# A two-block transformer kernel: the final norm of the first block folded into the second block's norm, and one of two attention maps weighed on VectorE instead of GpSimd

## What is computed

```python
# end of the first block
x = x + 0.5 * _swiglu(_rmsnorm(x, ffn2_norm), ffn2_w_gate, ffn2_w_up, ffn2_w_down)
x = _rmsnorm(x, final_norm)             # x * rsqrt(mean(x*x) + 1e-6) * gain
# start of the second block
h = _rms_norm(x, norm_g) * (1.0 + scale[:, None, :]) + shift[:, None, :]
dq, dk, dv, cq, ckv, kr, g = jnp.split(h @ w_in, cuts, axis=-1)
# its end
out = (mixed * jax.nn.silu(g)) @ w_out
return x + gate[:, None, :] * out
```

## Time and profile before

| what | value |
| --- | --- |
| median of 3 runs | 1967.73 us |
| the profiled execution: its own time | 1971.7 us |
| its span | 1969.9 us |
| mean granted TensorE clock | 0.961 |
| PE busy | 1844.2 us (94%) |
| DVE, ACT, POOL busy | 1042.8, 624.5, 97.8 us |
| first attention | about 518.5 to 716 us |
| last FFN matmul to the first slot's end | about 1523 to 1578 us |
| slots up to the second attention | to about 1750 us |
| gate and output projection | about 1858 to 1970 us |

### The profile page before, as it was taken

How to read it: one execution, slowest core, us unless ns; L and a number is a source line. 1 busy time by engine, 2 the same in 40 slices (tenths; PEclk the granted TensorE clock), 3 DMA queues, 4 the chain that set the end, 5 groups by cost and what they waited for, 6 DMA issues and landing times.

```text
span 1969.9 us, 22640 instructions
## 1 busy us (share of the span) xinstructions
PE 1844.2 (94%) x9109; PEld 1393.0 (71%) x9109; DVE 1042.8 (53%) x1597; ACT 624.5 (32%) x975; POOL 97.8 (5%) x148
## 2 busy tenths in 40 slices
PE   7999999999888899998999999999999499899888
PEld 6888888878555568755788888888887254365667
DVE  6665453465354445358644357534545655656753
ACT  4221221321256641024322233212223255324620
POOL 0000000000134420000000000000000000011100
PEclk8999998999699999999999999999999699799989
DMA  6545322362000012031333233233323022111221
GB/s 203 186 145 196 107 86 59 103 197 69 1 1 1 1 44 76 17 101 43 97 96 96 98 91 107 84 99 107 99 80 111 27 91 86 38 44 33 76 74 54
DMA packets 234908, 163.59 MB, mean 83 GB/s; under 512 B 10317, under 2 KB 225589, under 8 KB 234677
## 3 DMA queue, kind: packets, MB, share of 16 engines
q1 hardware_dynamic: 232484, 157.95, 26.3%
q10 hardware_dynamic: 2320, 4.20, 0.6%
HBM read 155.84 MB, written 6.29 MB: 82 GB/s over the span
## 4 chain that ended last, share of the span: by engine, by line
PE 83%; DVE 11%; issue 2%; POOL 2%; ACT 2%; DMA 0%; SPq 0%; ACTq 0%; DVEq 0%
PE bank L860 23%; PE bank L861 22%; PE bank L862 22%; PE bank L1070 2%; DVE bank L1745 2%; PE bank L1209 2%; POOL Pm L497 2%; PE bank L1060 2%; PE bank L1094 1%; DVE rout L1835 1%; PE bank L1155 1%; PE bank L1147 1%; PE bank L937 1%; PE bank L930 1%; PE bank L1324 1%
## 5 line engine op out<-in xcount | busy, mean ns | idle before, releaser
L860 PE MATMUL bank<-h_hi,w_hi 128*128 128x512 f32 x1216 | 492.4, 405 | 16.4 <-DVE h_lo L1467 12.3
L862 PE MATMUL bank<-h_hi,w_lo 128*128 128x512 f32 x1216 | 477.3, 393 | 0.0
L861 PE MATMUL bank<-h_lo,w_hi 128*128 128x512 f32 x1216 | 477.2, 392 | 0.0
L554 ACT ACTIVATE w_hi<-w_raw 128x2048 fp32r<-128x2048 f32 (+3 forms) x134 | 236.8, 1767 | 630.7 <-PE bank L862 567.8
L1404 DVE TENSOR_TENSOR w_lo<-w_raw,w_hi 128x2048 fp32r<-128x2048 f32 (+3 forms) x134 | 282.4, 2108 | 58.6 <-ACT w_hi L554 55.8
L860 PEld LDWEIGHTS bank<-h_hi,w_hi 128*128 128x128 f32 x1216 | 231.2, 190 | 94.0 <-issue 40.6
L861 PEld LDWEIGHTS bank<-h_lo,w_hi 128*128 128x128 f32 x1216 | 231.3, 190 | 53.0 <-issue 6.4
L862 PEld LDWEIGHTS bank<-h_hi,w_lo 128*128 128x128 f32 x1216 | 230.5, 190 | 49.3
L860 PE MATMUL bank<-u_hi,w_hi 128*128 128x512 f32 x352 | 138.0, 392 | 0.0
L861 PE MATMUL bank<-u_lo,w_hi 128*128 128x512 f32 x352 | 137.8, 392 | 0.0
L862 PE MATMUL bank<-u_hi,w_lo 128*128 128x512 f32 x352 | 137.6, 391 | 0.0
(11 more groups left out here) (352 smaller groups left out, 2548.4 us busy)
## 6 DMA issues: line engine op xcount, KB each, us to landing
w_raw<-in_w_in SPq DMA_DIRECT2D x28, 1024.0 KB, 5.2
w_raw<-in_ffn_w_gate SPq DMA_DIRECT2D x44, 512.0 KB, 3.7
w_raw<-in_ffn_w_up SPq DMA_DIRECT2D x44, 512.0 KB, 4.8
w_raw<-in_ffn_w_down SPq DMA_DIRECT2D x32, 704.0 KB, 4.5
ada_w<-in_ada_w SPq DMA_DIRECT2D x16, 768.0 KB, 6.3
w_raw<-in_w_in SPq DMA_DIRECT2D x21, 512.0 KB, 3.9
w_raw<-in_w_out SPq DMA_DIRECT2D x8, 1024.0 KB, 5.0
w_raw<-in_w_branch_nsa SPq DMA_DIRECT2D x8, 512.0 KB, 5.0
```

The lines of the kernel that those rows point to most:

```text
L554: act.activation(w_hi[s % 2][:, 0:n], w_raw[s % 2][:, 0:n], ACT.Copy).then_inc(s_hi, 1)
L860: pe.matmul(o, l[0], r[0], start=first, stop=False)
L861: pe.matmul(o, l[0], r[1], start=False, stop=False)
L862: return pe.matmul(o, l[1], r[0], start=False, stop=last)
```

## The change

**Part 1, the norm.** With g the final gain, e = 1e-6 and r the product of both inverse roots, r = 1/sqrt(mean((g*g+e)*x*x) + e*e). ACT therefore squares x times sqrt(g*g+e) (`G_ROOT`) first, then plain, then writes `xg` = x times gain times scale (`G_OUT`). From the weighted sum comes std = 1/r by one root, and DVE forms h = xg + std*shift, which is the wanted h times std. The projections behind it are linear, so their tiles are multiplied by r when they are emptied: `scale_tile` in place of `copy_tile` in slots 0 to 11, `scale_rows` for `dv`, and for the gate a DVE pass before ACT's silu. `xg` lies in the place of `h_lo`. The normed x itself, needed only at the end, is made in slots 2 (inverse root) and 10 to 17 (one `final_tile` each).

**Part 2, the bias matmuls.** The eight inside `first_tiles` move behind it, into slot 0.

**Part 3, the first attention.** POOL weighs the first map of a unit, DVE the second (`weigh_second`); `p_ready` comes after POOL's one instruction, and the transposes of the second map wait for a new signal `p1_ready`.

```diff
+G_EPS2, G_ROOT, G_OUT = 120, 0, 8
+        xg = at("xg", [P, KD, S], F32, base[0] - KD * S * 4)
...
                 pool.wait_ge(sem("sum_ready"), attended(u))
-                for i in range(2):
-                    p_ = Pm[u % 2][:, i, 0:n]
-                    ins = pool.tensor_scalar(p_, p_, mstat[:, u % 2, 6 + i:7 + i], gates[:, t, g0 + 3 * i:g0 + 3 * i + 1], ALU.mult, ALU.mult)
-                ins.then_inc(sem("p_ready"), 1)
+                p_ = Pm[u % 2][:, 0, 0:n]
+                pool.tensor_scalar(p_, p_, mstat[:, u % 2, 6:7], gates[:, t, g0:g0 + 1], ALU.mult, ALU.mult).then_inc(sem("p_ready"), 1)
... (ACT, square)
-                act.activation((sq_w if n == 2 else sq)[k % 2][:, :], x[:, k, :], ACT.Square).then_inc(sem("nsq"), 1)
                 if n == 3:
-                    act.activation(sqg[k % 2][:, :], x[:, k, :], ACT.Square, scale=col[:, G_FIN + k:G_FIN + k + 1]).then_inc(sem("nsqg"), 1)
+                    act.activation(sqg[k % 2][:, :], x[:, k, :], ACT.Square, scale=col[:, G_ROOT + k:G_ROOT + k + 1]).then_inc(sem("nsqg"), 1)
+                act.activation((sq_w if n == 2 else sq)[k % 2][:, :], x[:, k, :], ACT.Square).then_inc(sem("nsq"), 1)
+                if n == 3:
+                    act.activation(xg[:, k, :], x[:, k, :], ACT.Copy, scale=col[:, G_OUT + k:G_OUT + k + 1]).then_inc(sem("xg_ready"), 1)
... (ACT, big_norm(3))
+                    act.wait_ge(sem("gmm"), 1)
+                    act.activation(std[:, :], bank[6][:, :], ACT.Sqrt, bias=col[:, G_EPS2:G_EPS2 + 1], scale=1.0 / D).then_inc(sem("token_std"), 1)
... (ACT)
-            act.wait_ge(sem("gsum_ready"), 1)
-            act.activation(std[:, :], tmp[:, :], ACT.Sqrt, bias=col[:, G_EPS:G_EPS + 1], scale=1.0 / D).then_inc(sem("nstd"), 1)
... (ACT, zg)
-                act.wait_ge(acc_full, a + 1)
-                if i >= 2:
-                    act.wait_ge(acc_free, a - 1)
-                act.activation(gate_out[i % 2][:, :], bank[a % 4][:, :], ACT.Silu).then_inc(sem("zg_ready"), 1)
                 if i == 0:
                     norm_sqrt(26, 3, slice(0, P), 128)
+                act.wait_ge(acc_free, a + 1)
+                act.activation(gate_out[i % 2][:, :], gate_out[i % 2][:, :], ACT.Silu).then_inc(sem("zg_ready"), 1)
... (PE, turn)
                 for i in range(maps):
+                    if i:
+                        pe.wait_ge(sem("p1_ready"), attended(u))
... (PE, beside)
-                if slot < BIAS_SLOTS and slot:
+                if slot < BIAS_SLOTS:
                     bias_four()
-                if slot == 1:
+                if slot < 2:
                     bias_four()
+                if slot == 21:
+                    pe.wait_ge(sem("rs_ready"), 4)
+                    pe.wait_ge(sem("rope_done"), 22)
+                    for t in range(NT):
+                        ins = pe.matmul(bank[4][:, t:t + 1], rsx[0:1, t * P:(t + 1) * P], ones[0:1, 0:1], start=True, stop=True)
+                    ins.then_inc(sem("rst_full"), 1)
-                    first_tiles(wh, wl, ..., (h_hi, h_lo), ("h_ready", 24), bias_four)
+                    first_tiles(wh, wl, ..., (h_hi, h_lo), ("h_ready", 24))
... (DVE, final_norm)
-                dve.wait_ge(sem("nstd"), 4)
-                done(dve.reciprocal(rs[:, :], std[:, :]), "rs_ready")
-                dve.wait_ge(sem("gmm"), 1)
-                done(dve.tensor_mul(tmp[:, :], bank[6][:, :], rs[:, :]))
-                done(dve.tensor_mul(tmp[:, :], tmp[:, :], rs[:, :]), "gsum_ready")
-                final_tile(0)
-                dve.wait_ge(sem("nstd"), 5)
-                done(dve.reciprocal(rs2[:, :], std[:, :]), "rs_ready")
+                dve.wait_ge(sem("token_std"), 1)
                 for k in range(KD):
-                    if k:
-                        final_tile(k)
-                    done(dve.scalar_tensor_tensor(t, x[:, k, :], col[:, G_MOD + 8 + k:G_MOD + 9 + k], rs2[:, :], ALU.mult, ALU.mult))
-                    tick(dve.tensor_scalar(t, t, col[:, G_MOD + k:G_MOD + k + 1], None, ALU.add), "hn_ready")
+                    dve.wait_ge(sem("xg_ready"), k + 1)
+                    tick(dve.scalar_tensor_tensor(t, std[:, :], col[:, G_MOD + k:G_MOD + k + 1], xg[:, k, :], ALU.mult, ALU.add), "hn_ready")
                     if k:
                         low3(k - 1)
                 low3(KD - 1)
+                done(dve.reciprocal(rsx[:, :], std[:, :]), "rs_ready")
... (DVE, first attention)
+            def weigh_second(u):
+                dve.wait_ge(sem("sum_ready"), attended(u))
+                tick(dve.tensor_scalar(p_, p_, mstat[:, u % 2, 7:8], gates[:, t, g1:g1 + 1], ALU.mult, ALU.mult), "p1_ready")
                     sums(u, 2)
+                    weigh_second(u)
                 if u + 2 < U0:
                     peaks(u + 2)
... (DVE, evacuate)
-                copy_tile(dst, n)
+                if t is not None:
+                    scale_rows(dst, t, 256)
+                elif slot < 12:
+                    scale_tile(dst)
+                else:
+                    copy_tile(dst)
...
+                if slot == 2:
+                    dve.wait_ge(sem("nstd"), 4)
+                    done(dve.reciprocal(rsf[:, :], rsf[:, :]))
+                if 10 <= slot < 18:
+                    final_tile(slot - 10)
+                if slot == 21:
+                    dve.wait_ge(sem("rst_full"), 2)
+                    done(dve.tensor_copy(col[:, G_RST:G_RST + NT], bank[4][:, 0:NT]))
... (DVE, gate)
+            scale_tile(gate_out[0][:, :])
             inverse(5)
             for m in range(KD):
-                take()
+                if m + 1 < KD:
+                    scale_tile(gate_out[(m + 1) % 2][:, :])
                 dve.wait_ge(sem("zg_ready"), m + 1)
-                free(dve.tensor_mul(tmp[:, :], (diff_out + latent_out)[m], gate_out[m % 2][:, :]))
+                done(dve.tensor_mul(tmp[:, :], (diff_out + latent_out)[m], gate_out[m % 2][:, :]))
```

More of the change, by code:

```diff
@@ L588, in work @@
                 def work(i, a):
+                    if n == 3 and i == 1:
+                        act.wait_ge(sem("root_ready"), 1)
+                        act.wait_ge(sem("gain_out"), 2)
                     if i and n < 3:
@@ L598, in deviation @@
                     act.wait_ge(sem("rs_ready"), n)
-                act.activation((std_w if n == 2 else std)[:, :], bank[5][:, :], ACT.Sqrt, bias=col[:, G_EPS:G_EPS + 1], scale=1.0 / D).then_inc(sem("nstd"), 1)
+                act.activation((std, std, std_w, rsf)[n][:, :], bank[5][:, :], ACT.Sqrt, bias=col[:, G_EPS:G_EPS + 1], scale=1.0 / D).then_inc(sem("nstd"), 1)
             def big_norm(n):
@@ L666, in prepare @@
                     act.activation(cosM, ang[1][:, :], ACT.Sin).then_inc(sem("trig_ready"), 1)
+                if i == 17:
+                    act.wait_ge(sem("root_in"), 1)
+                    act.activation(col[:, G_ROOT:G_ROOT + KD], col[:, G_ROOT:G_ROOT + KD], ACT.Sqrt).then_inc(sem("root_ready"), 1)
             ffn("ffn1", 1)
@@ L900, in big_norm @@
             def big_norm(n):
+                if n == 3:
+                    pe.wait_ge(sem("sqg_added"), 7)
+                    pe.matmul(bank[6][:, :], ones, sqgsum[:, :], start=True, stop=True).then_inc(sem("gmm"), 1)
                 pe.wait_ge(sem("sq_added"), 7 * n + 7)
@@ L904, in big_norm @@
                 pe.matmul(bank[5][:, :], ones, (sqsum_w if n == 2 else sqsum)[:, :], start=True, stop=True).then_inc(sem("nmm"), 1)
-                if n == 3:
-                    pe.wait_ge(sem("sqg_added"), 7)
-                    pe.matmul(bank[6][:, :], ones, sqgsum[:, :], start=True, stop=True).then_inc(sem("gmm"), 1)
             def norm_sum(weights, quarter, start, stop, again=False):
@@ L1280, in _ @@
                 if s == 0:
-                    first_tiles(wh, wl, ((0, slice(0, P)), (0, slice(P, 2 * P))), (h_hi, h_lo), ("h_ready", 24), bias_four)
+                    first_tiles(wh, wl, ((0, slice(0, P)), (0, slice(P, 2 * P))), (h_hi, h_lo), ("h_ready", 24))
                     beside()
@@ L1423, in add_square @@
                 s_, t_ = (sq_w, sqsum_w) if n == 2 else (sq, sqsum)
+                dve.wait_ge(sem("dve_seq"), count.get("dve_seq", 0))
+                if n == 3:
+                    dve.wait_ge(sem("nsqg"), k + 1)
+                    done(dve.tensor_add(sqgsum[:, :], (sqg[0] if k == 1 else sqgsum)[:, :], sqg[k % 2][:, :]), "sqg_added")
                 dve.wait_ge(sem("nsq"), 8 * n + k + 1)
-                dve.wait_ge(sem("dve_seq"), count.get("dve_seq", 0))
                 if k > 1:
@@ L1429, in add_square @@
                 done(ins, "sq_added")
-                if n == 3:
-                    dve.wait_ge(sem("nsqg"), k + 1)
-                    done(dve.tensor_add(sqgsum[:, :], (sqg[0] if k == 1 else sqgsum)[:, :], sqg[k % 2][:, :]), "sqg_added")
             def tile_done(n, k):
@@ L1446, in final_tile @@
             def final_tile(k):
```

(13 more changed lines are left out.)

10 lines of the change are left out of this document (6 added, 4 removed).

## The result

The changed kernel takes 1934.34 us (median of 4 runs, 1933.61 to 1934.52) against 1967.62 us before (4 runs, 1966.37 to 1970.86): a ratio of 0.9827, 95% interval 0.9815 to 0.984. That is 33.3 us less, in a forecast of 1934 us with a range of 1924 to 1948. Its profiled execution took 1933.6 us with a span of 1931.8 us and a mean granted clock of 0.972. The two profiled spans lie 38.1 us apart, 4.8 us more than the medians.

What follows compares the result with a forecast made beforehand. PE, busy 94% of the span, was taken as the bound, so other engines' work counts only where PE idles. Attention -12, norm -26.5 and later costs +4.5 make -34.0 from 1967.7, rounded 1934 us, range 1924 to 1948.

Steps and rivals of the forecast that it cites:

- The deduction for the lock: First attention: contention between DVE's and POOL's weighing, 0.28 us for the held instruction, takes the gain from 15.0 to 12 us.
- DVE's cover: First attention: DVE's 88.9 us of waiting for scores, in 52 waits, hides its added 0.5 us a unit.
- PE's clock matters little here: Norm: first bias matmul comes at 1545.5 whether PE's first tiles run slow (end 1545.7) or fast (1541).
- Costs put later: Behind the norm, slots through gate: work moved or added there costs +4.5 us (+2 to +9).
- (c): Slots 10 to 17: `final_tile`, 0.75 us each, is hidden in waits except in slots 15 to 17: +1.3 us.
- (e): Gate: DVE's extra pass is hidden except at PE's stall before 1881.06, +0.7 us, and the last tile, +1.9.
- (d): Slot 21: four tiny matmuls and a copy of 0.15 us cost +0.6 us.
- eat the split: Rival, first attention: the port lock between DVE and POOL leaves a gain of 4 instead of 12, 1942 us; chance 0.13.
- stay slow behind the norm: Rival, bias matmuls: PE keeps its lower clock, so the norm gives 19 us, 1941 us in all; chance 0.13.
- become the bound in the slots: Rival, slots: inverse root and eight `final_tile` all fall on DVE's path, 8 us more, 1942 us; chance 0.05.
- More than I count: Rival, first attention: the clock may not fall, up to 4 us, and all 15 us of stalls come, 1927 us; chance 0.15.
- decided for slower: Rival, first attention: DVE's weighing, held by POOL to some 2.1 us, delays `peaks(u+2)`; 1987 us at 2.5 us; chance 0.02.

## Why the prediction was right

**The sum** was right to a microsecond, and in part by luck. With the stages averaged over the profiles that share their code it is -14.9 - 25.4 + 6.9 = -33.4 us, which is the medians' -33.3. The forecast was -12 - 26.5 + 4.5 = -34.0. The attention gave 2.9 us more than forecast; the norm gave 1.1 us less and the later costs were 2.4 us higher.

**Part 3: -12 forecast, 14.9 measured.** The mechanism was right: the stalls shrank. They shrank by 10.3 us, a little less than the 12 taken and well below the 15.0 of the upper end, and they stand at 21.2 us, just outside the "15 to 20" given as a sign. What the term lacked is the clock. It had been made a rival ("worth up to 4 us"), and it gave the other 4.6: over the attention PE was busy for 175.4 to 178.9 us in the four profiles that have the new one, and for 180.3 to 182.9 in the three with the old one, 4.9 us less between the means. Nine of fifteen late pairs had slow matmuls before and three of twenty have them now, at about 1.5 us each; an estimate from that is 3.3 us for five late pairs, and the rest is not located.

The deduction for the lock was of the right kind. POOL loses 0.06 to 0.27 us in each unit, 0.17 on average over the four widths; an estimate from that is 3 us in 18 stalls. The Trainium skill ("SBUF — State Buffer", "Who interferes with whom") calls the lock exclusive and its loser fully blocked. The trace agrees with the blocking: at all four widths POOL ends as long behind DVE as it needs alone, less 0.22 us. The cost is small because DVE's instruction is short and starts first, 0.06 us ahead, and because 0.22 us of POOL's own lie beside it.

**DVE's cover** was counted rightly: it gave 42 of 88.9 us, and the trace of the changed kernel shows no wait of PE for DVE's map in this attention.

**The norm: -26.5 forecast, -26.3 measured in the two profiles, -25.4 over all.** Its steps fell where they were forecast, relative to the last x update: the last h_lo done 16.1 us behind it (16.3 forecast), and the sixteen bias matmuls began 22.3 us behind it (22.5). They took 6.6 us where 5.3 had been worked out; the half microsecond set aside for a slower start covered part of that. "PE's clock matters little here" held: PE was slow for 2.7 us, until 1515.9, and had its eight k done before the step came. That the step sets the end, not h, was shown twice: by undoing part 2 (+10.3) and by making the steps first (-2.6).

**Costs put later: +4.5 forecast, +5.2 in the two profiles, +6.9 over all.** (c) is +1.4, and the run with `final_tile` moved showed it to be exactly that. (e) was right in what it named: 1.88 us more of pause at the last tile (4.58 for 2.70) and 0.60 for 0.7 at the stall. But the last stage grew by 3.7 us on average, and the 1.2 us beyond those pauses are not located; the two profiles of before differ there by 3.7 us too, with the same pauses and a granted clock of 0.97 and 0.99. (d) is the term that failed: "four tiny matmuls and a copy of 0.15 us: +0.6". The four are eight instructions in the trace and took 1.86 us, 0.23 each, about half the pitch of the 128x512 matmuls that follow them (0.43); the stage grew by 1.9. I priced them by the one column that they move, and left out what comes with each: it loads 128 columns of weights (`rsx` is the stationary operand), and PE's weight loads fill 1.78 of the 1.86 us.

**The rivals.** The lock did not eat the split (10 us of stalls, not 4). PE did not stay slow behind the norm in the changed kernel; with the bias matmuls inside it does, and at 1.03 us each. DVE did not become the bound in the slots. "More than I count" was right about the clock, and the attention gave 3 us more than forecast, not the 7 it would have had to, since the stalls gave 10 and not 15. The weighing that would have decided for slower, 2.1 us, was never above 0.55.

## What to carry to other kernels

Before splitting a step between two engines, ask which map the waiting engine takes first and which engine is the quicker for it: here the order of two transposes, or two DVE instructions in a row, gave 5 us more than DVE and POOL side by side with POOL's map first. Look at what stands ahead of the instruction that the bottleneck waits for on the same queue: moving 1.4 us of unhurried work from there was worth 9 to 14 us. Where stalls shrink, ask too whether the matmuls behind them were slow: here a third of the attention's gain was that. And a shorter chain pays only up to the next wait behind it, so cost the two together: of the 26 us at the norm, 10 needed the other edit.

## What the runs showed of the hardware that was not expected

- A GpSimd TENSOR_SCALAR that starts 0.06 us behind VectorE's like instruction (0.35 to 0.55 us) ends 0.23, 0.34, 0.45 and 0.55 us behind it at widths 128 to 512, its time alone less 0.22 us. So it grew by 0.06 to 0.27 us; VectorE's did not grow.
- The same code takes 21.83 or 22.85 us a head pair before and 20.51 or 21.97 after, by whether TensorE's matmuls behind a stall run at the lower clock. Single executions of before lie between 1962.8 and 1972.5 us.
- A transpose of one row to one column (1x128 to 128x1, float32) took 0.46 us on TensorE, as two instructions, in a stretch at the lower clock; its two loads of 128 columns of weights filled 1.78 of 1.86 us over four such transposes.
